# Running sums kept in on-chip memory, four PSUM places for the V products, turn-backs inside three groups

## The reference

```python
def peer_ffn(a, w_q, k1, k2, u, v):
    ...
    def block(args):
        xb, ib, gb = args
        ue = jnp.take(u, ib, axis=0)
        act = jax.nn.gelu(jnp.einsum('td,ted->te', xb, ue).astype(jnp.float32), approximate=False)
        ve = jnp.take(v, ib, axis=0)
        return jnp.einsum('te,ted->td', (gb * act).astype(xb.dtype), ve)
```

## Time and profile before

| | |
|---|---|
| time, median of 3 runs | 3639.81 us (3638.12 to 3640.16) |
| the profiled execution: time, span, mean granted TensorE clock | 3631.66 us, 3629.8 us, 0.976 |
| busy over the span: PE, DVE, POOL, ACT | 94%, 77%, 61%, 33% |
| stage V, 2520 to 3470 us: PE, DVE, POOL busy | 905.0, 824.8, 585.4 of 950 us |
| longest lines in the list of groups: `v` rows L1688, gathers of `v` rows L617 | 487.9 us, 391.5 us |

### The profile page before, as it was taken

One profiled execution on the slowest core, in us unless ns is written; L12 is line 12 of the kernel. 1 busy time (PEld: TensorE's weight loads), 2 busy tenths in 40 slices (PEclk: granted clock), 3 DMA queues, 4 the chain that ended last, 5 costly groups with the idle time before them and its releaser, 6 DMA issues. The chain is left out here.

```text
span 3629.8 us, 58833 instructions
## 1 busy us (share of the span) xinstructions
PE 3413.5 (94%) x22379; PEld 3345.2 (92%) x22379; DVE 2784.8 (77%) x4227; ACT 1197.4 (33%) x1873; POOL 2197.2 (61%) x1422
## 2 busy tenths in 40 slices
PE   7899989979999989999999999999999999999987
PEld 6799989879999979999999999999999999999976
DVE  5614467676787667999999998653888998988867
ACT  3310131213122232465656655542222222222232
POOL 5578864322688655666666666665666666666534
PEclk9999989989999999999999999999999999999988
DMA  4233432111598868788888888996988898988713
GB/s 150 84 116 122 139 106 72 49 48 58 184 315 312 281 215 300 276 308 310 312 324 314 319 297 316 319 350 224 322 312 310 307 315 313 315 311 310 263 33 103
DMA packets 326461, 856.08 MB, mean 236 GB/s; under 512 B 27792, under 2 KB 125584, under 8 KB 322960
## 3 DMA queue, kind: packets, MB, share of 16 engines
q0 software_dynamic: 110592, 402.70, 30.8%
q1 hardware_dynamic: 74592, 260.24, 21.5%
q10 hardware_dynamic: 141104, 190.87, 15.2%
HBM read 758.82 MB, written 94.90 MB: 235 GB/s over the span
## 5 line engine op out<-in xcount | busy, mean ns | idle before, releaser
L590 POOL TENSOR_TENSOR w_lo<-raw,w_hi 128x1024 fp32r<-128x1024 f32 x206 | 532.2, 2584 | 417.1 <-ACT w_hi L1053 412.1
L708 PE MATMUL main<-mix_hi,w_hi 128*128 128x320 f32 (+1 forms) x2816 | 684.4, 317 | 31.2 <-DVE mix_lo L1519 10.2
L708 PE MATMUL main<-mix_hi,w_lo 128*128 128x320 f32 (+1 forms) x2816 | 672.2, 313 | 0.0
L708 PE MATMUL main<-mix_lo,w_hi 128*128 128x320 f32 (+1 forms) x2816 | 672.2, 313 | 0.0
L617 POOL DMA_INDIRECT rows<-v_rows,s_idx x384 | 391.5, 1020 | 369.2 <-DVE scr L1688 297.5
L1688 DVE SCALAR_TENSOR_TENSOR scr<-rows,s_dot,scr 128x1024 f32<-128x1024 f32 x381 | 487.9, 1281 | 51.1 <-DMA rows<-v_rows,s_idx 39.9
L954 PE MATMUL main<-h_hi,v_hi 128*128 128x320 f32 x2048 | 474.5, 313 | 46.3 <-DVE res L2073 40.5
L708 PEld LDWEIGHTS main<-mix_hi,w_hi 128*128 128x128 f32 x2816 | 476.0, 189 | 35.9 <-issue 13.2
L708 PE MATMUL main<-a_hi,w_hi 128*128 128x320 f32 (+1 forms) x1728 | 466.7, 324 | 33.6 <-DVE a_lo L1519 8.9
L708 PEld LDWEIGHTS main<-mix_lo,w_hi 128*128 128x128 f32 x2816 | 479.8, 189 | 0.0
L617 POOL DMA_INDIRECT rows<-u_rows,s_idx x384 | 395.8, 1031 | 137.5 <-issue 69.8
(11 more groups left out here) (259 smaller groups left out, 5324.0 us busy)
## 6 DMA issues: line engine op xcount, KB each, us to landing
raw<-stream SPq DMA_DIRECT2D x478, 512.0 KB
act_d<-actb ACTq DMA_DIRECT2D x128, 320.0 KB
gate_d<-gbuf ACTq DMA_DIRECT2D x20, 2048.0 KB, 9.3
h<-act_d ACTq DMA_DIRECT2D x128, 320.0 KB
gate_in<-gate_d ACTq DMA_DIRECT2D x31, 1280.0 KB
rows<-u_rows,s_idx POOLq DMA_INDIRECT x384
rows<-v_rows,s_idx POOLq DMA_INDIRECT x384
score_d<-stage ACTq DMA_DIRECT2D x16, 320.0 KB
```

The costliest lines, as they stand in the source:

```text
L590: pool.tensor_tensor(w_lo[:, s, :], raw[:, s, :], w_hi[:, s, :].bitcast(F32), ALU.subtract) \
L708: last = pe.matmul(main[s][:, dst:dst + n], wt[:, s, c * P:(c + 1) * P], rows[:, c, src:src + n], start=(c == 0 and wt is w_hi and rows is ...
```

## The change

The running sums go to SBUF: `rows[13]` for blocks 0 and 2, `out0` for block 1. ScalarE's three copies go. `scr0` and `scr1` are then free in stage V, and a product takes one of four places, `main0`, `main1`, `scr0`, `scr1` by dt % 4. A sum is turned straight from SBUF into `scr1`, at dt 2 of groups 8, 22 and 31, and the product of dt 3, whose place is `scr1`, waits for `add_sparse`, which VectorE does after the drain of dt 1. Nothing else moves: no gather, no load, no order of the rows.

```diff
-ACC = (0, 1, 0)
+TURNS = {8: 0, 22: 1, NGRP - 1: 2}
+TURN_DT = 2
...
+        summed = [rows[13], out0, rows[13]]
...
-            pe.sem_inc(b_drained, 2)
+            pe.sem_inc(b_drained, 4)
...
-            def group(b, u, ahead_of=lambda dt: None):
+            slots = (main[0], main[1], scr[0], scr[1])
+
+            def turn_back(t):
+
+                pe.wait_ge(dot_done, UDOTS + P * (t + 1))
+                for c in range(DC):
+                    last = pe.transpose(scr[1][:, c * P:(c + 1) * P], summed[t][:, c * P:(c + 1) * P], ident[:, :])
+                last.then_inc(s_turned, 1)
+
+            def group(b, u, turn=None):
                 for dt in range(DC):
-                    ahead_of(dt)
-                    slot = main[dt % 2]
+                    slot = slots[dt % 4]
+                    if turn is not None and dt == TURN_DT:
+                        pe.wait_ge(b_drained, DC * b + 4)
+                        turn_back(turn)
+                    if turn is not None and dt == 3:
+                        pe.wait_ge(s_added, turn + 1)
                     pe.wait_ge(b_drained, DC * b + dt + 1)
...
-                if b == 5:
-                    act.wait_ge(dot_done, UDOTS + P)
-                    act.copy(out0[:, :], scr[0][:, :]).then_inc(s_out, 1)
-                if b == TURN_AT - 1:
-                    act.wait_ge(dot_done, UDOTS + 2 * P)
-                    act.copy(rows[13][:, :], scr[1][:, :]).then_inc(s_out, 1)
...
             act.wait_ge(dot_done, DOTS)
-            act.copy(rows[9][:, :], scr[0][:, :]).then_inc(s_out, 1)
...
                     if k < UDOTS:
                         acc = scr[(1, 0, 0)[t]]
                     else:
-                        acc = scr[ACC[t]]
+                        acc = summed[t]
...
                         if t == 1:
-                            dve.wait_ge(gates_drained, 32 * ND + 2)
+                            dve.wait_ge(tile_done, 2 * B_PAIR)
                         if t == 2:
-                            dve.wait_ge(s_out, 1)
+                            dve.wait_ge(s_turned, 1)
...
-                dve.tensor_tensor(r, main[dt % 2][:, :].rearrange("p (a t) -> p a t", a=2)[:, :, 0:HD], r, ALU.add) \
+                dve.tensor_tensor(r, (main + scr)[dt % 4][:, :].rearrange("p (a t) -> p a t", a=2)[:, :, 0:HD], r, ALU.add) \
```

More of the change, by code:

```diff
@@ L91 @@
 STAT_TURN = 2
-TURN_AT = 22
-LAST_TURN = 2
 NORM_TURN = 5
-ACC = (0, 1, 0)
+TURNS = {8: 0, 22: 1, NGRP - 1: 2}
+TURN_DT = 2
 LAST_ROWS = 2 * S1 + NE - 8
@@ L491, in build @@
         s_ready = sem("s_ready")
-        s_out = sem("s_out")
         s_turned = sem("s_turned")
@@ L679, in _ @@
                     .then_inc(tile_split, 1)
-            pool.wait_ge(s_added, 1)
+            pool.wait_ge(s_added, 2)
             for t in range(2 * DC):
@@ L962, in _ @@
                 pe.wait_ge(main_drained[s], B_PAIR + 1)
[L963 to L987, removed]
+            pe.wait_ge(dot_done, UDOTS)
+            pe.wait_ge(gates_drained, 32 * ND + 2)
+            at_group = 0
+            for turned in sorted(TURNS):
+                with pe.Fori(at_group // 2, turned // 2) as i:
+                    for u in range(2):
+                        group(2 * i + u, u)
+                for b in range(turned // 2 * 2, min(turned // 2 * 2 + 2, NGRP)):
+                    group(b, b % 2, TURNS.get(b))
+                at_group = turned // 2 * 2 + 2
+            pe.wait_ge(b_drained, DC * NGRP + 4)
             def ple_part(n):
@@ L1441, in _ @@
             for c in range(DC):
-                act.wait_ge(b_drained, DC * (NGRP - 1) + c + 3)
+                act.wait_ge(b_drained, DC * (NGRP - 1) + c + 5)
                 square(4, c, 2, res[:, c, :])
@@ L2079, in add_sparse @@
                 r = res[:, :, t * P:(t + 1) * P]
-                dve.tensor_tensor(r, scr[(1, 1, 0)[t]][:, :].rearrange("p (c t) -> p c t", c=DC), r, ALU.add) \
+                dve.tensor_tensor(r, scr[1][:, :].rearrange("p (c t) -> p c t", c=DC), r, ALU.add) \
                     .then_inc(s_added, 1)
@@ L2089, in _ @@
                     drain(b, dt)
+                    if dt == TURN_DT - 1 and b in TURNS:
+                        add_sparse(TURNS[b])
                     if 2 <= dt < 2 + EG:
@@ L2099, in _ @@
                     dot(share(share(B_DOTS, b, NGRP - 1), dt, DC))
-                if b in (TURN_AT + 1, TURN_AT + 3):
-                    add_sparse((b - TURN_AT) // 2)
             dot(DOTS - at_dot[0])
@@ L2108, in _ @@
                 drain(NGRP - 1, dt)
-                if dt == LAST_TURN - 1:
+                if dt == TURN_DT - 1:
                     add_sparse(2)
-                if dt >= LAST_TURN:
-                    add_square(4, dt - LAST_TURN, 2)
-            for c in range(DC - LAST_TURN, DC):
+                if dt >= TURN_DT:
+                    add_square(4, dt - TURN_DT, 2)
+            for c in range(DC - TURN_DT, DC):
                 add_square(4, c, 2)
```

## The result

The changed kernel takes 3682.11 us (median of 4 runs, 3678.45 to 3686.99) against 3639.85: ratio 1.0133, interval 1.0116 to 1.0149, so about 48 us slower; the two medians themselves differ by 42.3 us, the lower end of that interval. The forecast was 3684, with +48 for stage V, +3 for stage A and -5 at the edges.

The account below looks back on a forecast made before the run. A loop over GpSimd, a load, ScalarE and VectorE was taken to bind stage V, with TensorE following. 48 + 3 - 5 = +46 on the profiled 3631.7 gave 3678, 3686 with the runs' median, rounded to 3684; range 3655 to 3710.

Parts of the forecast that it names:

- +48 for stage V: Stage V: VectorE's `v` rows with sums in SBUF exclude GpSimd's work, lengthening the loop; +48 us over 29 groups, bounds 0 and +87.
- +3 for stage A: Stage A: 116 `v` rows meet `w_lo` splits, costing time at one place only; +3 us, bounds 0 and 10.
- -5 at the edges: Group 31 gives -2, the first two groups -2, and 1.5 us comes from the slack; together -5 us.
- the 1.46 us of slack: Start of group 14: fourth `h_lo` ends 1.46 us before TensorE needs it, so more places gain that once, not per group.
- the loop as I drew it: Stage V: chain over GpSimd split, load, ScalarE cast and VectorE, without a product; 29.27 us in group 13, mean 29.65.
- The hold: Stage V: a `v` row asks 0.14 us after its start and holds GpSimd off for 1.0 us.
- stretched by 1.67 us a group: Stage V: mean added loop time from `v` rows delaying gathers and splits, from three cases of +1.9, +1.0 and +2.2 us.
- the rival of the full VectorE: Stage V: each of four splits costs VectorE and the loop a full hold; 32.6 us a group, 3727 us; chance 0.13.
- one run of six rows: Stage A: 8.25 us run ahead of the one-hot matrices TensorE awaits; a split falling in adds up to 2.42 us.
- the -2 of group 31: Group 31: TensorE waits at dt 3, 1.5 + 1.2 us later, but has a product of 3.55 done; -2 us.
- The other 3 us, for the first groups and the slack: Stage V: the first two groups, with drains late by start-up, give -2 us; the slack of `h_lo` gives 1.5.
- the fast rival: Stage V: places were what was missing, TensorE's 32.0 us of drain waits go; 3600 us, loop under +0.15 a group; chance 0.16.

## Why the prediction was right, and where not

**The places.** Right: the wait for drains was a symptom. Four instead of two with sums in SBUF give 0.15%, the same without GpSimd's reads nothing (0.9924 and 0.9925), and each time TensorE's waits for drains turned into waits for `h_lo`, as worked out from the 1.46 us of slack. Three places with sums in PSUM give 1.0008, with the waits for drains still there. The reordered casts, -0.5% with the same places, show that the order of ScalarE's casts and the held `h_lo` are part of what sets the pace before the change. That the chain closes into the loop as I drew it is argued from the timeline of group 13; no run shows it link by link, and with the holding gone what TensorE's remaining waits come from was not followed.

**The sums.** The mechanism was right: bare length unchanged (1278 ns without readers), held when GpSimd reads, and gathers pushed back (median 940 to 1076 ns, mean 1238). Its price was forecast at +48 and is 50.2 in this profile, but that match is partly luck. Against the mean of the two profiles of the kernel before (909.7) it is 45, and what the times leave is less: 48 in all (42 by the medians), less the 9 of stage A, 33 to 40. So the term was probably too large, by anything from 3 to 15 us; the intervals do not say which. The hold, too, was a little smaller than worked out: the row above was stopped about 0.2 us after its start, where I had 0.14.

**What binds after it.** Here the working was off, though its sum held. I had the loop stretched by 1.67 us a group, with VectorE at 28.5 of 31.3 us. VectorE is busy 291.1 of 300, so 30.4 of 31.3, `h_lo`'s wait for ScalarE shrank from 21.9 to 13.3 us, and reordering the casts gives at most a little. That points to the rival of the full VectorE, at a much smaller price than I gave it (3727): each group has some 4.4 us of added holding (136 / 31) and became 1.7 us longer, so some 2.7 were covered by VectorE's idle time. That VectorE is the bound after the change is what these numbers suggest; no run gave VectorE less work there to show it. I had counted the `v` rows' holds and overlooked that the shifted splits meet h x gates more often: 1902 ns against 1287, or against 1531 in the second profile.

**Stage A.** The mis-sized term: +3, with bounds 0 and 10, measures 9 (0.26%), 10 by the starts of all profiles, and up to 13 in the pair with memsets in stage V alone. I had priced one run of six rows. It is there: it took 10.13 us instead of 8.25, and TensorE's wait after it is 4.82 instead of 4.14. But all 115 rows of that stretch go from 1287 to 1643 ns and its gathers from 1015 to 1356 in the kernel with the first sum alone in SBUF, which I had put down as covered. TensorE pays in more places than that one: in the changed kernel it waits twice for `hot` (6.9 us; once before, 4.1) and three times for `w_lo` (9.9 us; once, 7.2), from 2085 to 2530 us. That is 5.5 us of the 9; the rest was not located.

**Edges.** Of the -5, the -2 of group 31 did not come: after the last `v_lo` both kernels take 202 us (3685.2 - 3482.7, 3629.8 - 3427.5). My own figures did not give it either: a wait 1.5 + 1.2 us later with a product of 3.55 done is 0.85 us gained, not 2. In group 31 TensorE still waits 7.96 us, now at dt 3:

```profile
3513.00 0.90 PE L966 MATMUL scr<-h_hi,v_hi 128*128 128x320 f32 x2 [7.96 <-DVE res L2072]
```

The other 3 us, for the first groups and the slack, lie inside stage V, and no run separates them; four places against two gave 5 us there, not told from nothing.

Stage A came out 6 us above its term and group 31 2 above, stage V some us below: they nearly cancel, and the sum (46 forecast, 48 or 42 measured) is better than its terms. One threshold was also off: by its own inequality the fast rival needed less than 0.14 us a group, not 0.15. No chance hangs on that difference.

## What to carry to other kernels

A wait names the last link, not the bound: before buying a resource for it (a buffer, a PSUM place), follow the late engine back and see if the chain closes on itself without passing through the waiting engine. An operand in PSUM can be what keeps a VectorE instruction out of GpSimd's way; moving an accumulator to SBUF cost nothing by itself here, and 27% of each instruction where GpSimd subtracts beside it (1278 to 1622 ns). Order on a third engine (one cast ahead of another) was worth 0.5%, where one or two places more were worth nothing that could be measured. And a stage's length from one profile was good to 11 to 20 us in 900 here: price a change of that size by the times of several runs, or by several profiles.

## What was unexpected of the hardware

A GpSimd memset of 128x1024, which only writes, held no VectorE instruction with two SBUF inputs: 818 ns for h x gates with 372 memsets beside them, 1287 and 1531 in two profiles with 124 subtractions. A gather stands between: it is delayed by such instructions (mean 981 ns with sums in PSUM, 1146 with sums in SBUF, memsets in both), but with memsets and gathers alone no `v` row of stage V is held (1278 ns, at most 1287). The Trainium skill (SBUF — State Buffer, Who interferes with whom) has the first as its rule, and the trace agrees (818 ns); its inference, made for `tensor_tensor`, that such a VectorE instruction leaves descriptor writing alone does not carry over to these gathers (1146 against 981 ns). They also read their indices from SBUF (`s_idx`), so which part of a gather is delayed stays open.
